# Gate and up of two swiglu layers by seven half-size products, and the rest of a product ahead of the next weight split

## The chip, the core and the metric

The kernel runs on one core of a Trainium2 chip. The core has a matrix engine (PE, TensorE), a vector engine (DVE), an activation engine (ACT), a general engine (POOL, GpSimd) and a queue engine (SP) that issues most loads. The metric is the device time of one execution in microseconds; less is better.

## The reference, cut to what matters

Two blocks of a transformer over 512 tokens of width 1024, all in float32. The first block holds two swiglu layers of inner width 2816 around a mixer; the second has an even and an odd mixer, each followed by a squared-relu MLP of inner width 4096.

```python
def rmsnorm(x, g):
    y = xf * lax.rsqrt(jnp.mean(xf * xf, axis=-1, keepdims=True) + EPS)
    return (y * g)
def swiglu(h, w_gu, w_down):
    g, u = jnp.split(h @ w_gu, 2, axis=-1)
    return (jax.nn.silu(g) * u) @ w_down
# first block
x = x + 0.5 * rmsnorm(swiglu(rmsnorm(x, g_pre_ffn1), w_gu1, w_down1), g_post_ffn1)
x = x + mixer(...)
x = x + 0.5 * rmsnorm(swiglu(rmsnorm(x, g_pre_ffn2), w_gu2, w_down2), g_post_ffn2)
# second block, twice (even mixer, odd mixer)
x = x + mixer(...)
x = x + sq_relu_mlp(rmsnorm_2(x, norm_mlp), w_mlp1, w_mlp2)   # relu(h @ w1) ** 2 @ w2
```

## The kernel before, in words

**Tiling.** Activations stand as 128 features by 512 tokens a tile. Each float32 operand is kept in two parts, hi (rounded) and lo (the remainder), and a product of a 128x128 weight tile with an activation tile is three matmuls: hi by hi, lo by hi, hi by lo. In the code these are the three lines L2158, L2160 and L2162 (512 tokens each) for a whole product, and L2176, L2178 and L2180 (256 tokens each) for a half-size one.

**Weights.** The weights arrive in one stream, cut in chunks of mostly eight 128x128 tiles (128x1024). For each chunk ACT writes `whi` (L2463) and DVE writes `wlo` (L2807). The ring of these buffers has NW = 4 places, so the chunk at place c + 4 can be split only once the PE is done with the chunk at c. `opened(key)` puts the splits up to c + 3 into the order just ahead of the product on chunk c.

**A planner writes the order.** `work_order` builds one list of steps by hand-written loops; each engine executes its share of the list in that order, in order, with semaphore waits. What stands earlier in the list is therefore ahead on every engine.

**Swiglu layers** (`ffn`, key `gate`). A half layer has 11 gate and 11 up tiles, each one chunk of 8 k-tiles (24 matmuls of 512), then 8 down tiles of 11 k-tiles. The token factor of the norm, `rb`, is multiplied into gate and up on DVE (L2925, L2927), silu is on ACT (L2530), gate times up on POOL (L3332), the hi and lo parts of the result are written by ACT (L2533) and DVE (L2929). While half 0 runs, `extra` puts one step of the rotary tables between two pairs of tiles.

**MLP layers by seven** (`mlp`). In the two MLP layers of the second block, 28 of the 32 inner tiles are already computed in blocks of four tiles by seven products of half the tokens instead of eight: 8 k-slices by 3 matmuls of 256 tokens each. A block's products run in the order q1, p5, p6, q2, q7, then q1 of the next block, then q4 and q3. They need sums of token halves (`token_sums`, tiles `thi`, `tlo`: L2467, L2472 on ACT, L2818 to L2828 on DVE) and sums of weights (DVE L2811 and three accumulating loads by POOL L3326). Between products the result of one is copied out of its bank (`hold`, ACT L2481) or added to a held one (`corner_sum`, DVE L2839); a finished quarter (`corner`) goes through relu L2489, square L2492 and its hi part L2497 on ACT, and its lo part L2852 on DVE; for quarter c22 DVE does relu and square in one (L2845). p6 waits for q1's hold, q7 for p6's hold, q4 for the sum of c22, q3 for p5's hold. A half of an MLP layer runs three (half 0) or four (half 1) such blocks.

**The order inside a block before.** `multiplied` first calls `product`, which opens the chunk (so puts the next split) and puts the matmuls, and then `later()`, the rest of the product before (its corner work):

```python
at_once, then = product(f, name, (*afree, ...) if f == 12 else afree)
later()
...
at_once()
```

## Time and profile before

| | |
|---|---|
| runs | 2422.3, 2423.24, 2423.79 us |
| median | 2423.24 us |
| the profiled execution | 2421.31 us, of which the span is 2419.5 us |
| mean granted PE clock | 0.995 |
| PE busy | 2366.7 us, 98% |
| PE weight loads busy | 1945.0 us, 80% |
| DVE busy | 1327.2 us, 55% |
| ACT busy | 1064.4 us, 44% |
| POOL busy | 232.8 us, 10% |

The order of the stages is: swiglu f1 until about 375 us, the mixer until about 940, swiglu f2 until about 1311, the even mixer until about 1455, the MLP 0 until about 1800, the odd mixer, and the MLP 1 with products by seven at about 2080 to 2150 and 2235 to 2320. A busy share is an average: what a stage waits for is read in that stage, from its start times and from what an instruction's idle time before it ended with. A matmul's recorded duration is longer than its place in the pipeline; the pace is the distance of start times.

### The profile page before, as it was taken

How to read it: one execution, taken by the hardware profiler on the slowest of the kernel's cores; microseconds unless marked ns; L12 is line 12 of the kernel's file. 1: busy time of each engine (PE TensorE's matmuls, PEld its weight loads, DVE VectorE, ACT ScalarE, POOL GpSimd, SP SyncE). 2: the span in 40 equal slices, each digit the busy share in tenths (PEclk: the TensorE clock that was granted, in tenths of full speed). 3: DMA queues.
4: the chain of work that ended last, by engine and by line, in shares of the span. 5: the costliest groups of instructions: out<-in, count | busy, mean ns of one | idle time of the engine just before them, and what ended most of it. 6: DMA issues, size and time to landing. Idle time of an engine off the chain costs nothing.

```text
span 2419.5 us, 30917 instructions
## 1 busy us (share of the span) xinstructions
PE 2366.7 (98%) x12252; PEld 1945.0 (80%) x12252; DVE 1327.2 (55%) x2135; ACT 1064.4 (44%) x1759; POOL 232.8 (10%) x189
## 2 busy tenths in 40 slices
PE   9999999999999999999999999999999999999998
PEld 8888888777777788888887667989987677888987
DVE  5533436788654345433335866735645676753653
ACT  4323224455432334322323456624624785741642
POOL 0100100322102010100100200001000100100100
PEclk9999999999999999999999999999999999999999
DMA  4323223211122131323222215536522112644641
GB/s 153 99 87 104 99 84 102 84 53 53 62 70 73 55 118 62 113 86 106 96 86 88 82 46 133 148 105 157 140 96 64 38 48 67 163 122 123 162 117 69
DMA packets 72864, 230.68 MB, mean 95 GB/s; under 512 B 8080, under 2 KB 16528, under 8 KB 72464
## 3 DMA queue, kind: packets, MB, share of 16 engines
q1 hardware_dynamic: 66384, 206.34, 26.0%
q0 software_dynamic: 6048, 22.02, 5.5%
q8 instruction: 97, 1.59, 0.3%
q14 instruction: 47, 0.39, 0.0%
q10 hardware_dynamic: 288, 0.34, 0.0%
HBM read 226.57 MB, written 2.10 MB: 95 GB/s over the span
## 4 chain that ended last, share of the span: by engine, by line
PE 84%; DVE 6%; ACT 5%; issue 3%; DMA 2%; POOL 0%; POOLq 0%; DVEq 0%; ACTq 0%
PE bank L2158 21%; PE bank L2162 21%; PE bank L2160 21%; PE bank L2176 3%; PE bank L2178 3%; PE bank L2180 3%; PE bank L2342 2%; DMA wraw<-in_stream 2%; ACT whi L2463 2%; PE bank L2304 1%; PE bank L2349 1%; DVE wlo L2807 1%; PE bank L2249 1%; PE bank L2245 1%; PE bank L2247 1%
## 5 line engine op out<-in xcount | busy, mean ns | idle before, releaser
L2807 DVE TENSOR_TENSOR wlo<-wraw,whi 128x1024 fp32r<-128x1024 f32 (+3 forms) x462 | 518.0, 1126 | 552.4 <-ACT whi L2463 551.6
L2463 ACT ACTIVATE whi<-wraw 128x1024 fp32r<-128x1024 f32 (+3 forms) x462 | 435.1, 948 | 470.4 <-PE bank L2162 377.0
L2158 PE MATMUL bank<-hhi,whi 128*128 128x512 f32 x1288 | 514.7, 400 | 2.3 <-ACT hhi L2508 1.0
L2162 PE MATMUL bank<-hhi,wlo 128*128 128x512 f32 x1288 | 504.1, 391 | 1.6 <-DVE wlo L2807 1.5
L2160 PE MATMUL bank<-hlo,whi 128*128 128x512 f32 x1288 | 503.3, 391 | 0.4 <-DVE hlo L2858 0.4
L2158 PEld LDWEIGHTS bank<-hhi,whi 128*128 128x128 f32 x1288 | 242.2, 188 | 56.6 <-issue 6.7
L2162 PEld LDWEIGHTS bank<-hhi,wlo 128*128 128x128 f32 x1288 | 241.7, 188 | 56.0 <-DVE wlo L2807 4.1
L2160 PEld LDWEIGHTS bank<-hlo,whi 128*128 128x128 f32 x1288 | 242.4, 188 | 50.0 <-DVE hlo L2858 2.6
L2160 PE MATMUL bank<-mlo,whi 128*128 128x512 f32 x448 | 176.8, 395 | 0.2 <-DVE mlo L3164 0.2
L2158 PE MATMUL bank<-mhi,whi 128*128 128x512 f32 x448 | 176.9, 395 | 0.0
L2162 PE MATMUL bank<-mhi,wlo 128*128 128x512 f32 x448 | 176.9, 395 | 0.0
L2176 PE MATMUL bank<-hhi,whi 128*128 128x256 f32 x448 | 126.9, 283 | 1.3 <-DVE tmps L2839 1.0
L2180 PE MATMUL bank<-hhi,wlo 128*128 128x256 f32 x448 | 126.9, 283 | 0.9 <-DVE wlo L2807 0.9
L2178 PE MATMUL bank<-hlo,whi 128*128 128x256 f32 x448 | 126.7, 283 | 0.0
L3332 POOL TENSOR_TENSOR tmps<-tmps 128x512 f32<-128x512 f32 x44 | 56.6, 1286 | 612.0 <-DVE tmps L2927 464.6
L2160 PEld LDWEIGHTS bank<-mlo,whi 128*128 128x128 f32 x448 | 84.2, 188 | 20.3 <-DVE mlo L3164 0.5
L2162 PEld LDWEIGHTS bank<-mhi,wlo 128*128 128x128 f32 x448 | 84.2, 188 | 20.1
L2158 PEld LDWEIGHTS bank<-mhi,whi 128*128 128x128 f32 x448 | 84.2, 188 | 19.8 <-ACT mhi L2659 0.4
L2176 PE MATMUL bank<-thi,whi 128*128 128x256 f32 x336 | 95.9, 285 | 1.8 <-ACT whi L2463 1.6
L2180 PE MATMUL bank<-thi,wlo 128*128 128x256 f32 x336 | 95.3, 284 | 1.5 <-DVE wlo L2807 1.5
L2645 ACT ACTIVATE tmps<-bank 128x512 f32<-128x512 f32 x88 | 52.8, 599 | 99.6 <-PE bank L2342 97.9
L2178 PE MATMUL bank<-tlo,whi 128*128 128x256 f32 x336 | 95.1, 283 | 0.0
(459 smaller groups left out, 4224.6 us busy)
## 6 DMA issues: line engine op xcount, KB each, us to landing
wraw<-in_stream SPq DMA_DIRECT2D x335, 512.0 KB, 3.4
wraw<-in_stream POOLq DMA_DIRECT2D x34, 512.0 KB, 6.0
wraw<-in_stream SPq DMA_DIRECT2D x32, 192.0 KB, 2.3
wraw<-in_stream SPq DMA_DIRECT2D x22, 256.0 KB, 2.6
rot_tables<-in_stream SPq DMA_DIRECT2D x8, 512.0 KB, 5.5
rot_tables<-in_stream POOLq DMA_DIRECT2D x8, 512.0 KB, 5.5
wraw<-in_stream SPq DMA_DIRECT2D x26, 128.0 KB, 2.0
wraw<-in_stream SPq DMA_DIRECT2D x8, 320.0 KB, 2.9
```

Source lines behind the costliest of these rows:

```text
L2158: pe.matmul(out, sh, xh, start=first, stop=False)
L2160: pe.matmul(out, sh, xl, start=False, stop=False)
L2162: p = pe.matmul(out, sl, xh, start=False, stop=end and last)
L2176: pe.matmul(out, sh, xh, start=fresh and n == 0, stop=False, skip_group_check=True)
L2178: pe.matmul(out, sh, xl, start=False, stop=False, skip_group_check=True)
L2180: p = pe.matmul(out, sl, xh, start=False, stop=n == 7, skip_group_check=True)
L2245: pe.matmul(out, xh, sh, start=k == 0, stop=False)
L2342: p = pe.transpose(banks[tb][:, i * 128:i * 128 + 128], src[:, at0:at0 + 128], ident[:, :])
L2463: act.activation(whi[j][:, 0:L], src[:, 0:L], F.Copy).then_inc(*hi.up(c))
L2645: act.activation(et_of(stage, et)[:, c * 128:(c + m) * 128], banks[tb][:, 0:m * 128], F.Copy).then_inc(*turned.up((stage, u, c)))
L2807: dve.tensor_tensor(wlo[j][:, 0:L], src[:, 0:L], whi[j][:, 0:L].bitcast(f32), SUB).then_inc(*lo.up(c))
L3332: pool.tensor_tensor(tmps[:, q, :], tmps[:, q, :], tmps[:, u, :], MUL).then_inc(*gated.up((s, f)))
```

## The change

**Swiglu layers.** Of the 22 gate and 22 up tiles of a layer, 4 pairs (`PLAIN` = 0, 1, 2, 11) stay whole products and come first; the other 18 pairs (`GATED`) are computed in 9 blocks of two gate and two up tiles by the seven half-size products of the MLP layers, in the same order of products. The token sums are made during the plain tiles, before the first block. `by_seven` holds what the MLP and swiglu layers share. Per block there is one DVE addition of weights and three accumulating POOL loads. The factor `rb` is multiplied into gate only (`gate_in`, `glu_gate`, DVE); up stays unscaled, and the later norm gets the factor through its EPS term, `eps_x` (both norms after the swiglu). silu stays on ACT; gate times up is on DVE for half of the tokens (`glu_first`) and on POOL for the other half (`glu_second`), where before all of it was on POOL. The steps of the rotary tables move from f1's half 0 to the down tiles of its half 1.

**All layers by seven, the two MLP layers too.** `multiplied` now calls `later()` ahead of `product`, so the rest of the product before stands ahead of the next split on ACT and on DVE.

On the PE 10481 rows become 11777: 1296 more, which is 2 layers by 9 blocks by (168 - 96).

```diff
+PLAIN, GATED = (0, 1, 2, 11), ((3, 5, 7, 9), (12, 14, 16, 18, 20))
...
-    def ffn(tag, gu, down):
+    def ffn(s, tag, gu, down_of):
+        lows[s], least = [], len(plan) + 2
+        for f in PLAIN:
+            col(tag + "g", gu + "g", f)
+            col(tag + "u", gu + "u", f)
...
-    ffn("f1", "gu1", "down1")
...
+            seven(tag + "s", s, GATED[half], lambda f: quadrants([gu + "g"] * 2 + [gu + "u"] * 2, (f, f + 1) * 2), down,
+                  least)
+            down(99)
+        order, n = [f for fs in GATED for f in fs], 0
+        for f, low in zip(order, lows[s]):
+            if f in (GATED[0][0], GATED[1][0]):
+                plan[CH_of(tag + "s", f, "p5") - 4].then.append(low)
+            elif f == GATED[0][1]:
+                plan[CH_of(tag + "s", order[n - 1], "p5")].then.insert(0, low)
+            else:
+                plan[CH_of(tag + "s", order[n - 1], "p6")].then.append(low)
+            n += 1
+    def CH_of(*key):
+        return [chunk.key for chunk in plan].index(key)
...
-    def gate(s, f, tg, tu, afree):
-        q, u = T.take(), T.take()
-        put("gate", s, f, tg.bank, tu.bank, q.i, u.i, tg.end, tu.end, (*q.was, *u.was), afree)
+    def gate_in(s, f, tg):
+        q = T.take()
+        put("gate_in", s, f, tg.bank, q.i, tg.end, q.was)
         tg.freed(("g_scaled", (s, f)))
-        tu.freed(("u_scaled", (s, f)))
-        u.free = (("gated", (s, f)),)
+        return q
+    def gate_up(s, f, tu, q):
+        put("gate_up", s, f, tu.bank, q.i, tu.end)
+        tu.freed(("combined", ("gated", s, f)))
+    def gate_low(s, f, q, afree):
+        put("gate_low", s, f, q.i, afree)
         q.free = (("v_lo", (s, f)),)
...
-    def ffn(s, tag, nxt, natural, afree, yfree, extra):
...
+    def by_seven(s, tag, afree_of, corner, first_time=None):
...
+        def product(f, name):
+            key = (s, f)
...
+            c = opened((tag, f, name))
+            put("seven", s, name, c, b.i, was, fresh)
+            closed.add(c)
+            done = ("used", c)
...
+            return at_once, lambda: corner(f, name, b, bank[f, "q"] if name != "q4" and (f, "q") in bank else None, done,
+                                           afree_of(f))
+        def multiplied(fs, tiles, owed):
...
+            for f, name in products(fs):
+                if name == "down":
+                    next(tiles[0])
+                    next(tiles[0])
+                    later()
+                    later = nothing
+                    continue
+                later()
+                at_once, then = product(f, name)
+                if first_time and (f, name) == first_time[0:2]:
+                    put(*first_time[2])
+                at_once()
+                state["held"] = False
+                later = then
+                if not first_time or f > first_time[0]:
+                    next(owed, int)()
+            next(tiles[1])
+            next(tiles[1])
+            later()
+            return ("used", CH[(tag, fs[-1], "q3")])
+        return multiplied
+    def ffn(s, tag, nxt, natural, guard, yfree, extra):
...
-        sy = None
+        afree, sy = guard, None
+        silu_of, wait_lo = {}, []
+        def corner(f, name, b, q, done, free):
+            key = (s, f)
+            if name == "q2":
+                silu_of[f] = q
+                put("glu_gate", key, "c11", q.i)
+            elif name == "q7":
+                silu_of[f, "up"] = q
+            elif name == "q4":
+                q = silu_of[f]
+                put("glu_first", key, b.i, q.i, done, free)
+                b.free = (("combined", (key, "c21")),)
+                wait_lo.append((key, "c21", q))
+            elif name == "q3":
+                u = silu_of[f, "up"]
+                put("glu_gate", key, "c12", q.i)
+                put("glu_second", key, q.i, u.i)
+                low()
+                u.free = (("gated", (key, "c12")),)
+                wait_lo.append((key, "c12", q))
+            elif name == "p6":
+                low()
+        def low():
+            if wait_lo:
+                key, part, q = wait_lo.pop(0)
+                put("glu_low", key, part, q.i, afree)
+                q.free = (("v_lo", (key, part)),)
+        multiplied = by_seven(s, tag + "s", lambda f: afree, corner)
         for half in range(2):
...
-                                              fresh=s > 0)
-                g2 = run(feat([(tag + "g0", 2, 0)], ("h", s)))
+                g0, u0, g1, u1 = side_by_side(("h", s), *[(tag + c, n, 0) for n in range(2) for c in "gu"], fresh=s > 0)
+                token_sums(s, 0, guard)
+                token_sums(s, 1, guard)
+                g2 = run(feat([(tag + "g", 2, 0)], ("h", s)))
                 R.step()
-                gate(s, 0, g0, u0, afree)
-                gate(s, 1, g1, u1, afree)
...
+                q0, q1 = gate_in(s, 0, g0), gate_in(s, 1, g1)
+                gate_up(s, 0, u0, q0)
+                gate_up(s, 1, u1, q1)
+                q2 = gate_in(s, 2, g2)
+                gate_low(s, 0, q0, afree)
+                gate_low(s, 1, q1, afree)
+                u2 = run(feat([(tag + "u", 2, 0)], ("h", s)))
+                token_sums(s, 2, guard)
+                gate_up(s, 2, u2, q2)
+                gate_low(s, 2, q2, afree)
+                g3 = run(feat([(tag + "g", 11, 0)], ("h", s)))
+                token_sums(s, 3, guard)
+                q3 = gate_in(s, 11, g3)
+                u3 = run(feat([(tag + "u", 11, 0)], ("h", s)))
+                put("token_last", s, u3.end)
+                gate_up(s, 11, u3, q3)
+                gate_low(s, 11, q3, (("p_lo", ("last token", s)),))
...
+            begun = [tile(0), tile(1)]
+            h_end = multiplied(GATED[half], begun, iter(()))
+            while wait_lo:
+                low()
...
-                tiles = feat([(tag + f"d{half}", n, k0) for k0, _ in groups(11)], ("v", s, half * 11))
+                if half and n < 5:
+                    next(extra, None)
+                    next(extra, None)
+                tiles = begun[n] if n < 2 else tile(n)
...
-            put("rotary", n)
+            put("rotary", n, (("lo", CH["f1s", GATED[1][-1], "q7"]), *ang.was, *kq.was) if n == 0 else ())
...
-        def multiplied(fs, tiles, afree):
-            def nothing():
-                pass
-            later = nothing
...
-                    continue
-                at_once, then = product(f, name, (*afree, *open_sums["h", s].tok) if f == 12 else afree)
...
-                    put("token_last", s, ("used", CH[(f"m{l}u", 3, 0)]))
-                at_once()
-                state["held"] = False
-                later = then
-                if f > 4:
...
+        multiplied = by_seven(s, f"m{l}s", lambda f: (*afree, *open_sums["h", s].tok) if f == 12 else afree, corner,
+                              (4, "p5", ("token_last", s, ("used", CH[(f"m{l}u", 3, 0)]))))
...
+            eps_x = lsm[:, 32:36]
...
                     w.wait_ge(*var[norm])
+                    if norm in (("h", 0), ("h", 2)):
+                        dve.tensor_scalar(eps_x, v, EPS, None, MUL).then_inc(*chain.up())
...
                     last_norm = norm
-                    dve.tensor_scalar(v, banks[b][:, 0:4], 1.0 / n, EPS, MUL, ADD).then_inc(*var.up(norm))
+                    if norm in (("y", 0), ("y", 2)):
+                        dve.scalar_tensor_tensor(v, banks[b][:, 0:4], 1.0 / n, eps_x, MUL, ADD).then_inc(*var.up(norm))
...
+                elif k == "gate_up":
+                    s, f, b, q, end = a
+                    w.wait_ge(*at(end))
+                    w.wait_ge(*silu[s, f])
+                    dve.tensor_tensor(tmps[:, q, :], banks[b][:, :], tmps[:, q, :],
+                                      MUL).then_inc(*combined.up(("gated", s, f)))
...
+                elif k == "glu_gate":
+                    key, part, q = a
+                    w.wait_ge(*rbm["h", key[0]])
+                    w.wait_ge(*combined[key, part])
+                    dve.tensor_tensor(two(tmps[:, q, :]), two(tmps[:, q, :]), twice_rb(part),
+                                      MUL).then_inc(*g_scaled.up((key, part)))
+                elif k == "glu_first":
+                    key, b, q, done, afree = a
+                    w.wait_ge(*at(done))
+                    w.wait_ge(*silu[key, "c11"])
+                    dve.scalar_tensor_tensor(tmps[:, q, :], banks[b][:, :], -1.0, tmps[:, q, :], MUL,
+                                             MUL).then_inc(*combined.up((key, "c21")))
...
-                    w.wait_ge(*silu[s, f])
-                    w.wait_ge(*u_scaled[s, f])
+                elif k == "glu_second":
+                    key, q, u = a
+                    w.wait_ge(*silu[key, "c12"])
+                    w.wait_ge(*combined[key, "c22"])
                     w.wait_ge(*before.now())
```

In this diff the ACT parts of the steps are left out: `gate_in` and `glu_gate` are silu, `gate_low` and `glu_low` write the hi part (L2630 to L2645 of the changed kernel), as before. In the changed kernel the line numbers of common steps are: split L2563 (ACT) and L2921 (DVE), hold L2581, corner L2589, L2592, L2597, plain copy for token sums L2567, `thi` L2572, `rb` L2617.

**ACT in MLP 0, one block by seven, from the product after q2 on.** L2489, L2492, L2497 are relu, square and hi part of a corner, L2463 is a split and L2481 a hold; `mhi0` is the hi part of the MLP's inner tiles. Before:

```order
L2463 ACTIVATE whi3<-wraw0_1 128x1024
L2489 ACTIVATE tmps<-tmps 128x512
L2492 ACTIVATE tmps<-tmps 128x512
L2497 ACTIVATE mhi0<-tmps 128x2x256
L2463 ACTIVATE whi0<-wraw0_0 128x1024
L2497 ACTIVATE mhi0<-tmps 128x2x256
L2481 ACTIVATE ftmps<-bank 128x512
L2463 ACTIVATE whi1<-wraw0_0 128x1024
L2463 ACTIVATE whi2<-wraw0 128x1024
L2489 ACTIVATE tmps<-bank 128x512
L2492 ACTIVATE tmps<-tmps 128x512
L2497 ACTIVATE mhi0<-tmps 128x2x256
```

After, with L2589, L2592, L2597 for the corner, L2563 for a split, L2581 for a hold:

```order
L2589 ACTIVATE tmps<-tmps 128x512
L2592 ACTIVATE tmps<-tmps 128x512
L2597 ACTIVATE mhi0<-tmps 128x2x256
L2563 ACTIVATE whi1<-wraw0_1 128x1024
L2597 ACTIVATE mhi0<-tmps 128x2x256
L2563 ACTIVATE whi2<-wraw0_0 128x1024
L2581 ACTIVATE ftmps<-bank 128x512
L2563 ACTIVATE whi3<-wraw0_0 128x1024
L2589 ACTIVATE tmps<-bank 128x512
L2592 ACTIVATE tmps<-tmps 128x512
L2597 ACTIVATE mhi0<-tmps 128x2x256
```

The split of q3's chunk stood ahead of the corner of q2 and now stands behind it; the splits of p5 and of p6 of the next block stood together behind the hold of q1, and now p5's stands ahead of that hold, with the corner of c22 ahead of it.

**ACT in f1, from the first plain tiles on.** L2530 is silu with its table load, L2533 the hi part, L2517 the copy of `rb`. Before:

```order
L2463 ACTIVATE whi2<-wraw0 128x1024
L2463 ACTIVATE whi3<-wraw1 128x1024
L2517 ACTIVATE rb<-bank 128x512
L2530 ACT_TABLE_LOAD
L2530 ACTIVATE tmps<-tmps 128x512
L2533 ACTIVATE f1ahi<-tmps 128x512
L2530 ACTIVATE tmps<-tmps 128x512
L2533 ACTIVATE f1ahi<-tmps 128x512
L2463 ACTIVATE whi0<-wraw0 128x1024
L2530 ACTIVATE tmps<-tmps 128x512
L2533 ACTIVATE f1ahi<-tmps 128x512
```

After, from the third of four steps of token sums to the first hold (L2630 silu, L2636 hi part, L2567 and L2572 token sums, L2577 the last token sums' hi part):

```order
L2567 ACTIVATE tmps<-xa,cols 128x512 x2
L2572 ACTIVATE f1thi<-ftmps 128x3x256
L2636 ACTIVATE f1ahi<-tmps 128x512
L2563 ACTIVATE whi1<-f1wraw_0 128x1024
L2567 ACTIVATE tmps<-xa,cols 128x512 x2
L2572 ACTIVATE f1thi<-ftmps 128x3x256
L2630 ACTIVATE tmps<-tmps 128x512
L2563 ACTIVATE whi2<-f1wraw_0 128x1024
L2577 ACTIVATE hhi<-f1t4 128x4x256
L2636 ACTIVATE f1v11hi<-tmps 128x512
L2563 ACTIVATE whi3<-wraw0 128x1024
L2581 ACTIVATE ftmps<-bank 128x512
```

Two steps of token sums, a split, the copy of `rb`, the table load, three silus, two hi parts and the split of q1's chunk stand ahead of the first row of this piece. The first hold of a block (q1's, its last row) stands behind all four steps of token sums and behind the hi part of the last plain tile.

## Rows read from the trace of the kernel before

**Rows 1.** The page: busy us (share of the span) and instructions.
```profile
PE 2366.7 (98%) x12252; PEld 1945.0 (80%) x12252; DVE 1327.2 (55%) x2135; ACT 1064.4 (44%) x1759; POOL 232.8 (10%) x189
```

**Rows 2.** Windows: stretch, PE, PEld, DVE, ACT, POOL busy, clock, DMA share, GB/s.
```profile
1080.00:1140.00 60.00, 60.00 (x260) 48.52 (x259) 15.64 (x16) 17.26 (x23) 0.00 (x0) 1.00 0.34 108
1680.00:1740.00 60.00, 60.00 (x479) 58.83 (x478) 40.16 (x46) 41.08 (x57) 4.35 (x5) 1.00 0.64 160
```

**Rows 3.** Matmul groups: ns min/median/max, first and last start us (f2 down tiles).
```profile
L2158 PE MATMUL bank<-f2ahi,whi x176: 392/394/398, 1068.1 to 1310.3; 128*128 128x512 f32 x176
```

**Rows 4.** The same view, half-size products of MLP 0, half 1.
```profile
L2176 PE MATMUL bank<-hhi,whi x128: 277/283/283, 1653.5 to 1738.9; 128*128 128x256 f32 x128
L2176 PE MATMUL bank<-thi,whi x96: 279/282/285, 1656.4 to 1727.6; 128*128 128x256 f32 x96
```

**Rows 5.** Timeline of DVE, MLP 0 half 1: start us, us, instruction, idle before it.
```profile
1685.76 0.68 DVE L2839 TENSOR_TENSOR tmps<-bank,ftmps 128x512 f32<-128x512 f32 x1
...
1689.42 1.23 DVE L2807 TENSOR_TENSOR wlo<-wraw,whi 128x1024 fp32r<-128x1024 f32 x1 [0.66 <-ACT whi L2463]
1690.57 1.22 DVE L2811 TENSOR_TENSOR wraw<-wraw,wraw 128x1024 f32<-128x1024 f32 x1
1691.70 0.69 DVE L2845 SCALAR_TENSOR_TENSOR tmps<-tmps 128x512 f32<-128x512 f32 x1
```

**Rows 6.** Timeline of ACT, the same stretch.
```profile
1686.48 0.64 ACT L2489 ACTIVATE tmps<-tmps 128x512 f32<-128x512 f32 x1
...
1688.35 1.04 ACT L2463 ACTIVATE whi<-wraw 128x1024 fp32r<-128x1024 f32 x1
1692.42 0.63 ACT L2497 ACTIVATE mhi<-tmps 128x512 fp32r<-128x512 f32 x1 [3.03 <-DVE tmps L2845]
1692.96 0.58 ACT L2481 ACTIVATE ftmps<-bank 128x512 f32<-128x512 f32 x1
1693.43 2.00 ACT L2463 ACTIVATE whi<-wraw 128x1024 fp32r<-128x1024 f32 x2
1695.33 0.59 ACT L2489 ACTIVATE tmps<-bank 128x512 f32<-128x512 f32 x1
```

**Rows 7.** Matmul groups of MLP 0, half 0.
```profile
L2176 PE MATMUL bank<-thi,whi x72: 279/282/415, 1498.8 to 1558.4; 128*128 128x256 f32 x72
```

**Rows 8.** Timeline of DVE in MLP 0, half 0.
```profile
1513.12 0.68 DVE L2839 TENSOR_TENSOR tmps<-bank,ftmps 128x512 f32<-128x512 f32 x1
...
1546.14 0.15 DVE L2872 TENSOR_SCALAR sm<-bank 128x4 f32<-128x4 f32 x1
...
1548.19 1.22 DVE L2807 TENSOR_TENSOR wlo<-rot_tables,whi 128x1024 fp32r<-128x1024 f32 x1
```

**Rows 9.** Groups of DVE instructions in 1513 to 1556 us: busy us, mean ns.
```profile
L2863 DVE TENSOR_TENSOR ssb<-ssb,xa 128x512 f32<-128x512 f32 x7 | 4.8, 683 | 0.0
```

**Rows 10.** Timeline of PE and windows, MLP 0 half 0: a wait, and the clock behind it.
```profile
1543.94 1.05 PE L2268 MATMUL bank<-ones,ssb 128*128 128x1 f32 x8 [1.50 <-DVE ssb L2863]
...
1546.00:1549.00 3.00, 3.00 (x18) 0.56 0.97 225
```

**Rows 11.** Timeline of ACT and PE at the start of f1, and of ACT in f2.
```profile
32.61 1.06 ACT L2463 ACTIVATE whi<-wraw 128x1024 fp32r<-128x1024 f32 x1 [3.11 <-DMA wraw<-in_stream]
...
39.90 1.28 ACT L2530 ACT_TABLE_LOAD   x1
...
39.00 0.48 PE L2158 MATMUL bank<-hhi,whi 128*128 128x512 f32 x1
...
970.01 1.06 ACT L2463 ACTIVATE whi<-wraw 128x1024 fp32r<-128x1024 f32 x1 [3.11 <-DMA wraw<-in_stream]
...
975.50 0.48 PE L2158 MATMUL bank<-hhi,whi 128*128 128x512 f32 x1
```

**Rows 12.** Timeline of ACT, token sums of MLP 0.
```profile
1484.44 1.32 ACT L2467 ACTIVATE tmps<-ya,cols 128x512 f32<-128x512 f32 x2
...
1487.68 1.05 ACT L2463 ACTIVATE whi<-wraw 128x1024 fp32r<-128x1024 f32 x1
```

More of the change, by code:

```diff
@@ L173, in stream_plan @@
             add(("eo", n, half), "e_out", 4 * half, 4, n * 128, 128)
-    def CH_of(*key):
-        return [chunk.key for chunk in plan].index(key)
     def mlp(l):
@@ new lines, in gate_up, with token_sums @@
+    def gate_up(s, f, tu, q):
[3 more added lines that the diff above has]
+        put("gate_low", s, f, q.i, afree)
+        q.free = (("v_lo", (s, f)),)
+    first, both = FT.slots
+    def token_sums(s, k, guard):
+        qs = [T.take(), T.take()]
+        for q, j in zip(qs, (k, k + 4)):
+            put("plain", s, j, q.i, (*q.was, *x_at[j]))
+        put("token_sums", s, k, qs[0].i, qs[1].i, (*first.free, *both.free), guard)
+        for q in qs:
+            q.free = (("combined", ("token", s, k, 4)),)
+        put("token_parts", s, k, guard)
+        first.free = both.free = (("p_hi", ("token", s, k)), ("p_lo", ("token", s, k)))
@@ new lines, in ffn, with tile @@
+                token_sums(s, 3, guard)
[4 more added lines that the diff above has]
+                gate_low(s, 11, q3, (("p_lo", ("last token", s)),))
+            def tile(n):
+                return feat([(tag + f"d{half}", n, k0) for k0 in (0, 8)], ("v", s, half))
+            begun = [tile(0), tile(1)]
+            h_end = multiplied(GATED[half], begun, iter(()))
@@ L967, in work_order @@
     last, owed = None, 0.0
-    first, second = ([dil_unit(p, i) for i in range(4)] for p in range(2))
-    for unit in first + [None] + second + [None]:
+    ones_of, twos_of = ([dil_unit(p, i) for i in range(4)] for p in range(2))
+    for unit in ones_of + [None] + twos_of + [None]:
         pace = 1 if unit else 5
@@ L1182, in mlp @@
         put(*lows[s][0])
-        first, both = FT.slots
         def square(t, f, afree):
@@ L1189, in square @@
             q.free = (("v_lo", (s, f)),)
-        def token_sums(k):
-            qs = [T.take(), T.take()]
-            for q, j in zip(qs, (k, k + 4)):
-                put("plain", s, j, q.i, (*q.was, *x_at[j]))
-            put("token_sums", s, k, qs[0].i, qs[1].i, (*first.free, *both.free), guard)
-            for q in qs:
-                q.free = (("combined", ("token", s, k, 4)),)
-            put("token_parts", s, k, guard)
-            first.free = both.free = (("p_hi", ("token", s, k)), ("p_lo", ("token", s, k)))
         def one_more_split():
@@ new lines, in corner @@
+        def corner(f, name, b, q, done, free):
+            part = {"q2": "c11", "q7": "c22", "q4": "c21", "q3": "c12"}.get(name)
+            if part is None:
+                if name == "p6":
+                    low()
+                return
+            key = (s, f)
+            if part == "c21":
+                q = T.take()
+                put("corner", key, part, b.i, q.i, (done, *q.was), free)
+                b.free = (("relu_sq", (key, part, "relu")),)
+            else:
+                put("corner", key, part, None, q.i, (), free)
+            low()
+            wait_lo.append((key, part, q))
@@ L2022, in three, with twice_rb @@
             return v.rearrange("q (n t) -> q n t", n=3)
+        def twice_rb(part):
+            p = slice(0, 256) if part in ("c11", "c21") else slice(256, 512)
+            return rb[:, p].unsqueeze(1).to_broadcast([128, 2, 256])
         def two(v):
@@ L2027, in corner_of @@
         def corner_of(s, f, part):
-            f0, p = f % 16 + (2 if part in ("c11", "c12") else 0), slice(0, 256) if part in ("c11", "c21") else slice(256, 512)
-            a, b = v_tile(s, f0, 2)
+            p = slice(0, 256) if part in ("c11", "c21") else slice(256, 512)
+            if s < 3:
+                a, b = (v[:, f % 11:f % 11 + 2, :] for v in ahl[s])
+            else:
+                a, b = v_tile(s, f % 16 + (2 if part in ("c11", "c12") else 0), 2)
             return a[:, :, p], b[:, :, p]
```

208 lines of the change are left out of this document (99 added, 109 removed).

## The prediction

> **What bounds the kernel now.** First the page: the PE is busy 98% of the span, DVE 55%, ACT 44% [rows 1]. Fewer PE instructions' time should then shorten the kernel one for one, as long as ACT and DVE keep up where work is added to them. So I read two windows next. In the down tiles of f2 the weight loads fill 48.5 of 60 us and ACT 17 us; in a stretch of products by seven in MLP 0 the weight loads fill 58.8 and ACT and DVE 41 and 40 of 60 us [rows 2]. That is two thirds busy, yet their work is a chain: ACT writes a hi part, DVE the lo part, and each in its order. Whether such a chain fits into a block is the question in both kinds of layer. The timelines of the two engines in that stretch give its steps.
>
> **The PE's gain.** The pace of a 512-token matmul is (1310.3 - 1068.1) / 1053 = 0.2300 us, where 1053 is the intervals between: 176 groups of three on f2's down tiles and the 22 tiles of 24 of half 1 that stand among them, 528 + 528 - 3 [rows 3]. For half-size products, 224 groups of three stand between 1653.5 and 1738.9, 669 intervals, with 24 whole matmuls among them: (85.4 - 24 x 0.23) / 669 = 0.1194 us [rows 4]. A block of two gate and two up tiles is 96 x 0.2300 = 22.08 us before and 168 x 0.1194 = 20.06 us after, 2.02 less. Times 18 blocks: **-36.4 us**. A product by seven is 24 x 0.1194 = 2.87 us.
>
> The trace shows 0.2300 and 0.1194 us a matmul at a granted clock of 1.00 [rows 2 to 4]. The Trainium skill ("TensorE: Matmul & The Clock Gate", Back-to-back issue gap) gives a gap of N / 2.4 + 2.5 ns, so 215.8 and 109.2 ns. By that page's figures a block would go from 20.72 to 18.34 us and the gain would be an estimated 42.8 us, 6.4 more. The rows here are 7% and 9% above it, so the trace differs and decides.
>
> **The MLP layers: the order of corner and split.** Nothing is added there, but in the order of ACT the corner of a product now stands ahead of the next split. I walked one block with the intervals of the rows, from the sum of c11 on DVE (behind q2). Sum to relu 0.72 (1685.76 to 1686.48), relu, square and hi part to the next split 1.87 (to 1688.35) [rows 5, 6]. Split to its lo part on DVE 1.07 (to 1689.42), lo part to the next DVE work 1.15 (to 1690.57) [rows 5, 6]. Now the sum of c22: it stood in front of that lo part in time before, and now comes behind it. To its square 0.63, to the hi part on ACT 0.72 (1691.70 to 1692.42), to the split of p5's chunk 0.54, to its lo part 1.07, to the addition of weights 1.15, addition to the split of p6's chunk 1.25 (its 1.22 and a signal), that split 0.95 (a half of the pair's 1.90, 1693.43 to 1695.33), corner of c21 and the split of q2's chunk 1.87, its lo part 1.07, sum of c12 1.15, relu 0.72, corner and split of q7's chunk 1.87, next 0.95, the hold of p5 0.48 (1692.96 to 1693.43), the split of the next q1 to its lo part 1.07, that lo part, the lo part of a corner and one more weight's lo part 1.15 + 0.60 + 1.15, and the next sum of c11 is there. The sum is **23.2 us a block, in which the PE does not occur, against 20.06 us of the PE**. Before, the splits of p5 and p6 were issued together (the pair at 1693.43) and q3's ahead of the corner [rows 6], and the PE held the pace.
>
> In half 1 (four blocks) the way from the first sum of c11 to the last q7 is two blocks and, to the end of the hold of p6, 18.75 + 0.48 + 0.95 + 0.5 = 20.7: 2 x 23.2 + 20.7 = 67.1 against 3 x 20.06 = 60.2, so +6.9 in each MLP. In half 0 (three blocks) the first sum of c11 stands at 1513.12 [rows 8]. One block and 20.7 lead to 1557.0. Seven additions of squares (0.60 of place each, 4.2) and the root of the norm (1546.14 to 1548.19, 2.05) also stand on DVE there [rows 8, 9]; of these 6.25 I put 4.7 on the way, for those that stand between a lo part and the sum behind it: 1561.7. Before, the last product on token sums began at 1558.4 - 23 x 0.1194 = 1555.7 [rows 7]. So +6.0. Two MLPs: 2 x (6.9 + 6.0) = **+25.8 us**. The bounds: 0, if ACT has hidden time that the walk counts as bound, and 2 x (9.3 + 7.5) = 33.6 if nothing of the slack at the start of a half is there.
>
> **The clock.** Behind a wait of 1.50 us of the PE in MLP 0 the granted clock is 0.56 for 3 us [rows 10], that is a time at 1.2 GHz; about 1.3 us are lost. New stalls of 2 to 3 us a block can do this again; I take it twice, **+2.6 us** (0 to 12 x 1.3 = 15.6).
>
> **The swiglu blocks in their steady run.** The same walk with the work of a swiglu block: there is no relu and square pair, c21 and c12 need one DVE multiplication and one silu or none, and the hi parts are written a product later. It comes to about 19.3 us, under 20.06, so the PE holds the pace with 0.8 us in hand: 0. If that is lost, it is a rival (below). On POOL `glu_second` waits for the silu of c12, and behind it in POOL's order stand the accumulating loads of the next block's weight sums; what they feed is split three products (8.6 us) later, so I cost that wait at nothing too, and at a split that comes late if silu were over 8 us late.
>
> **The first block of each swiglu layer.** Here ACT has the four token steps as well. The last split before is at 32.61 [rows 11]. A token step takes 3.24 us on ACT, with its wait for DVE (1484.44 to 1487.68) [rows 12]. From 33.56, two steps lead to 40.0, a split to 41.0, the copy of rb to 41.6, the table load (1.28) [rows 11] to 42.9. Three silus, each between a DVE multiplication with rb and one with up, and two hi parts lead to the split of q1's chunk at 47.2; the third step and a hi part to p5's split at 53.7; lo part and addition end at 57.1, the fourth step and the last silu at 61.3, where p6's chunk is split; the last token sums' hi part 62.2; the hi part of tile 11, which waits for DVE and the end of the last up tile, 65.3; q2's split 65.9; then q1's hold, 66.8 to 67.4. The PE: the up tile 2 starts at 39.00 [rows 11], three tiles of 24 x 0.23 lead to 55.5, q1 and p5 to 61.2. p6 needs q1's hold: a stall of 6.2 us. In f2 the split is at 970.01 and the up tile at 975.50 [rows 11]: 5.49 apart instead of 6.39, so 7.1 us. Together **+13.3 us**. The bounds: ACT's work alone is five splits, four steps, silus, hi parts and the copies, an estimated 25.6 us by the durations of rows 6, 11 and 12, to 59.2 from 33.56 on, which would be no stall; with every wait it is 8 us a layer.
>
> **The rest** I cost at nothing. EPS times the variance is one DVE instruction on 4 columns a layer, like the one of 0.15 us that opens a root [rows 8]. The rotary steps move to down tiles, where ACT and DVE have 17 and 16 of 60 us of work [rows 2], so they are covered; uncovered, five double steps would be a few us. 18 more additions of weights and 54 accumulating loads: MLP 0 runs the same at a DMA share of 0.64 [rows 2].
>
> **The sum**, against the profiled execution: 2421.3 - 36.4 + 13.3 + 2.6 + 25.8 = 2426.6. The median of the runs is 1.9 above the profiled one (2423.24 against 2421.31): **2428 us**.
>
> **The rivals.** (a) The MLP walk is too long: ACT and DVE run ahead at the block's start and the PE keeps its pace; only the start stalls stay. 2421.3 - 36.4 + 13.3 + 2.6 + 1.9 = 2403. For it speaks that ACT and DVE are two thirds busy [rows 2]; against it that every step of the walk is a row. 0.12. (b) The MLPs bind, but the first blocks' stalls are hidden, since the waits for DVE are shorter than walked: 2428 - 13.3 - 1.3, about 2413. 0.18. (c) Neither binds: 2387. 0.04. (d) Slower: the swiglu loop, 0.8 us under the PE's pace in my walk, is over it by 0.8 us on average, as two signals of 0.8 would do; 16 blocks x 0.8, and the clock falls in some of them: 2428 + 15 = 2443. It decides from a chain over 20.06 us a block. For it: the two loops differ by four instructions only. 0.14.
>
> **How the numbers follow.** The forecast, 2428 with its own range of 2419 to 2438, has 0.52. From 2404 to 2441 no more than 2 in 10 is left out: most of (a) is at the lower edge, half of (d) is above. A measurement here can tell 0.2%, 4.8 us: faster is under 2418.4: (a), (c) and most of (b), 0.31. Within: 2418.4 to 2428.1, half of the forecast and the rest of (b), 0.31. Slower: the other half and (d), 0.38.
>
> **What would show it.** In f2's blocks, L2276 starts 20.1 us a block apart and no idle time of the PE. In MLP 0's half 1, blocks 23 us apart, the PE idle twice a block, ended by ACT's hold (L2581) and by DVE or ACT behind the sum of c22; ACT's rows between with short idle times ended by DVE. At about 61 us and 997 us one idle time of the PE of 6 to 7 us, ended by ACT L2581. The clock row near 1.00 elsewhere. The forecast is wrong if MLP 0's half 1 takes 85 us as before, or if the f1 blocks are over 20.5 us each.

## The result and the profile after

The changed kernel takes 2485.12 us, the kernel before 2423.24 us: a ratio of 1.0253, 95% interval 1.0241 to 1.0264. It is 62 us slower where 5 us slower was forecast, and outside the range.

The page of the changed kernel, in its first row, the row of its second DMA queue and the row of the chain that ended last, by engine; below it the same row of the kernel before:

```profile
PE 2366.4 (95%) x13548; PEld 2004.4 (81%) x13548; DVE 1470.2 (59%) x2287; ACT 1158.9 (47%) x1892; POOL 245.7 (10%) x217
...
q0 software_dynamic: 13824, 50.34, 11.7%
...
PE 69%; DVE 10%; ACT 9%; DMA 6%; issue 6%; POOL 0%; POOLq 0%; ACTq 0%; DVEq 0%
```

```profile
PE 84%; DVE 6%; ACT 5%; issue 3%; DMA 2%; POOL 0%; POOLq 0%; DVEq 0%; ACTq 0%
```

The PE was at 98% [rows 1] and is at 95%: 117 us without it, where there were 53. Its busy time is the same to 0.3 us although it has less to do: part of it runs at the lower clock. The share of DMA in the chain went from 2% to 6%, and those of DVE and ACT nearly doubled. The second row is the queue of the accumulating loads: 50 MB, 22 MB before.

Where the time went can be read from the starts of one group of matmuls that both programs have at every norm (L2279 before, L2379 after): at the end of f1 378.06 before and 385.54 after, at the end of f2 1314.56 and 1329.12. The stretches are cut at these starts.

| stretch | before, us | after, us | difference |
|---|---|---|---|
| f1 | 339.87 | 347.40 | +7.5 |
| the first block's mixer | 563.93 | 562.63 | -1.3 |
| f2 | 372.57 | 380.95 | +8.4 |
| even mixer's norm | 33.08 | 33.13 | 0 |
| even mixer and MLP 0 | 486.92 | 513.14 | +26.2 |
| odd mixer and MLP 1, half 0 | 296.76 | 306.86 | +10.1 |
| MLP 1 to its last norm | 277.79 | 290.25 | +12.5 |

The two swiglu layers, which were to gain, lost 16 us, and the stretches of the two MLP layers, which had their order changed only, 49 us. Two kinds of wait stand in the PE's timeline after (start, duration, instruction, idle time before it and what ended it), at the start of a swiglu layer, in a steady swiglu block, and in MLP 0, half 1:

```profile
67.56 0.55 PE L2276 MATMUL bank<-f1thi,whi 128*128 128x256 f32 x1 [5.47 <-ACT ftmps L2581]
...
1011.37 0.55 PE L2276 MATMUL bank<-f2thi,whi 128*128 128x256 f32 x1 [5.45 <-ACT ftmps L2581]
...
102.79 0.36 PE L2276 MATMUL bank<-hhi,whi 128*128 128x256 f32 x1 [1.91 <-DVE tmps L2953]
...
125.01 0.36 PE L2276 MATMUL bank<-hhi,whi 128*128 128x256 f32 x1 [1.93 <-DVE tmps L2953]
...
274.65 0.36 PE L2276 MATMUL bank<-hhi,whi 128*128 128x256 f32 x1 [2.85 <-DVE tmps L2953]
...
1723.26 0.55 PE L2276 MATMUL bank<-hhi,whi 128*128 128x256 f32 x1 [4.73 <-DVE tmps L2953]
...
1749.78 0.55 PE L2276 MATMUL bank<-hhi,whi 128*128 128x256 f32 x1 [4.78 <-DVE tmps L2953]
```

The first two are q1's hold, the start stall of the prediction. The others are q4 waiting for the sum of c22 (L2953). In the MLP they were forecast, at some 3 us a block. In the steady swiglu blocks they were not, and 11 of them leave the PE idle for 18.0 us. They cost an estimated 20 us: idle time is counted from the recorded end of a matmul, 0.28 us after its start, and the pace is 0.12 us, so each wait costs some 0.16 us more than it shows. The chain that ended last in the MLP explains both. Its pieces from one such wait to the next, in order of time (start, us, what):

```profile
1696.43 0.69 DVE tmps L2953
1697.15 0.70 DVE tmps L2959
1697.90 0.52 issue
1698.41 1.05 ACT whi L2563
1699.53 1.10 issue
1700.63 1.23 DVE wraw L2925
...
1704.76 0.96 ACT whi L2563
1705.74 1.24 DVE wlo L2921
1707.00 8.38 DMA wraw<-in_stream
1715.40 1.07 ACT whi L2563
1716.53 1.11 issue
1717.63 0.69 DVE tmps L2953
```

This is my walk of one block, sum of c22 to split of p5, to the addition, to the split of q2's chunk and its lo part. But behind the lo part there is not the sum of c12: there is a load of 8.38 us. In the code of the plan, the weight tiles b (of q2) and d (of q4) of a block use the same raw buffer in turn. When DVE has written the lo part of q2's chunk, SP may load d, and d must have landed for the split of q4's chunk, three products (8.6 us) later in the order. From q2's lo part to the next sum of c11 it is 11.9 us (1705.74 to 1717.63) this way, where my way over the sum of c12, two splits and a hold had 9.1. A block takes 26.5 us (1749.78 less 1723.26). ACT, which works in order, waits for the load:

```profile
1715.40 1.06 ACT L2563 ACTIVATE whi<-wraw 128x1024 fp32r<-128x1024 f32 x1 [2.96 <-DMA wraw<-in_stream]
1718.35 0.63 ACT L2589 ACTIVATE tmps<-tmps 128x512 f32<-128x512 f32 x1 [1.89 <-DVE tmps L2953]
```

The chain in f1 has the same load, between 86.41 and 95.50 us (9.1 us) and again between 109.03 and 117.72 (8.7 us). Over that stretch of the MLP the median load of 512 KB by SP lands after 3.7 us; the one in the chain takes over twice that.

The kernel before has this load too. It is issued at 1696.91, beside the accumulating loads of its block, and lands at 1703.65, after 6.7 us. ACT's split waits for it, but only briefly, and the PE not at all:

```profile
1703.67 1.06 ACT L2463 ACTIVATE whi<-wraw 128x1024 fp32r<-128x1024 f32 x1 [0.67 <-DMA wraw<-in_stream]
```

### The profile page after: what moved, and what is told of

It reads as the page before. It is cut to its first block, busy times and chain, and to the rows that moved or that the text cites. A ratio compares the mean times of both kernels' runs of the same rounds, so it can differ in the third digit from the quotient of the medians.

```text
span 2483.9 us, 33903 instructions
## 1 busy us (share of the span) xinstructions
PE 2366.4 (95%) x13548; PEld 2004.4 (81%) x13548; DVE 1470.2 (59%) x2287; ACT 1158.9 (47%) x1892; POOL 245.7 (10%) x217
## 4 chain that ended last, share of the span: by engine, by line
PE 69%; DVE 10%; ACT 9%; DMA 6%; issue 6%; POOL 0%; POOLq 0%; ACTq 0%; DVEq 0%
PE bank L2258 15%; PE bank L2262 15%; PE bank L2260 15%; DMA wraw<-in_stream 6%; PE bank L2276 4%; ACT whi L2563 4%; PE bank L2280 4%; PE bank L2278 4%; DVE wlo L2921 2%; PE bank L2442 2%; DVE tmps L2953 1%; PE bank L2404 1%; PE bank L2449 1%; PE bank L2349 1%; PE bank L2345 1%
## 5 line engine op out<-in xcount | busy, mean ns | idle before, releaser
L2921 DVE TENSOR_TENSOR wlo<-wraw,whi 128x1024 fp32r<-128x1024 f32 (+4 forms) x442 | 496.0, 1124 | 528.3 <-ACT whi L2563 527.5
L2563 ACT ACTIVATE whi<-wraw 128x1024 fp32r<-128x1024 f32 (+4 forms) x442 | 415.6, 943 | 424.7 <-PE bank L2262 262.5
L2276 PE MATMUL bank<-hhi,whi 128*128 128x256 f32 x1024 | 300.4, 293 | 50.3 <-DVE tmps L2953 45.3
L2280 PE MATMUL bank<-hhi,wlo 128*128 128x256 f32 x1024 | 297.9, 291 | 1.0 <-DVE wlo L2921 1.0
L2278 PE MATMUL bank<-hlo,whi 128*128 128x256 f32 x1024 | 298.1, 291 | 0.0
L2258 PE MATMUL bank<-hhi,whi 128*128 128x512 f32 (+1 forms) x712 | 290.9, 409 | 1.7 <-ACT hhi L2608 1.0
L2262 PE MATMUL bank<-hhi,wlo 128*128 128x512 f32 (+1 forms) x712 | 280.1, 393 | 3.4 <-DVE wlo L2921 3.4
L2260 PE MATMUL bank<-hlo,whi 128*128 128x512 f32 (+1 forms) x712 | 279.2, 392 | 0.4 <-DVE hlo L2972 0.3
L2258 PEld LDWEIGHTS bank<-hhi,whi 128*128 128x128 f32 (+1 forms) x712 | 134.1, 188 | 34.0 <-issue 5.4
L2260 PEld LDWEIGHTS bank<-hlo,whi 128*128 128x128 f32 (+1 forms) x712 | 134.3, 189 | 27.6 <-DVE hlo L2972 2.9
```

The source lines that it names most:

```text
L2258: pe.matmul(out, sh, xh, start=first, stop=False)
L2260: pe.matmul(out, sh, xl, start=False, stop=False)
L2262: p = pe.matmul(out, sl, xh, start=False, stop=end and last)
L2276: pe.matmul(out, sh, xh, start=fresh and n == 0, stop=False, skip_group_check=True)
L2278: pe.matmul(out, sh, xl, start=False, stop=False, skip_group_check=True)
L2280: p = pe.matmul(out, sl, xh, start=False, stop=n == 7, skip_group_check=True)
```

## The experiments

**Theory A**: the order is the cause; with the corner ahead of the split, each lo part comes later, and the reload of d closes a loop over both engines and the queue. **Theory B**: the added work in the swiglu layers binds whatever the order. **Theory C**: the reload is long only because the accumulating loads of the same moment share the DMA engines with it.

**e1: the old order everywhere.**

```diff
-                later()
                 at_once, then = product(f, name)
+                later()
```

> The changed kernel with the order of before in all layers by seven: product (and its split) first, then the rest of the product before. Theory A (the order of corner and split closes a loop through the raw buffer's reload, in swiglu and MLP alike): the MLPs lose the 48.8 us they gained, the steady stalls of the swiglu blocks go, the two stalls of 6 to 7 us at their start stay with their clock: 2423.2 - 36.4 + 13.3 + 5 = about 2405 us. Theory B (in the swiglu layers the added ACT, DVE and load work binds whatever the order): the MLPs come back, the swiglu layers stay 16 us longer than before: about 2437 us.

Measured: 2422.73 us, ratio 1.0003 (0.9993 to 1.0012). The MLPs came back (MLP 0's stretch 487.3 us, before 486.9), and the waits for the sum of c22 in the swiglu blocks went. So the order was the MLP loss, but for 3 us (from the end of f2 to the last norm 1097.3 us, before 1094.6). But the swiglu layers reached only 2.3 us under before, not 18. What is left there is the start stall, as in the changed kernel, and at four of f1's and five of f2's blocks a wait of over 0.5 us of this kind:

```profile
67.61 0.55 PE L2276 MATMUL bank<-f1thi,whi 128*128 128x256 f32 x1 [5.47 <-ACT ftmps L2581]
...
260.02 0.36 PE L2276 MATMUL bank<-f1thi,whi 128*128 128x256 f32 x1 [0.92 <-ACT ftmps L2581]
```

It lies between A's 2405 and B's 2437, and neither holds as it stood: A is right on the large waits, and the small ones, which stay in the old order, it did not have.

**e2: the new order alone, in the kernel before.**

```diff
-                at_once, then = product(f, name, (*afree, ...) if f == 12 else afree)
                 later()
+                at_once, then = product(f, name, (*afree, ...) if f == 12 else afree)
```

> The kernel before with one edit: in the two MLP layers the rest of a product stands ahead of the next split; swiglu layers as before. Theory A: the whole MLP loss of the changed kernel, +48.8 us: about 2472 us, with waits of some 4.8 us of the PE a block for the sum of c22. My prediction's walk alone (ACT and DVE, no load in the loop) says +28: 2451 us. If the MLP loss came from something the swiglu part changed (buffers, tables, placing), no change: 2423 us.

Measured: 2464.6 us, ratio 1.017 (1.0154 to 1.0186), +43 us. The two lines do by themselves nearly all that the MLPs lost; my walk without a load (+28) is too short by 15 us. The waits are those of the changed kernel:

```profile
1705.22 0.55 PE L2176 MATMUL bank<-hhi,whi 128*128 128x256 f32 x1 [4.72 <-DVE tmps L2839]
```

**e3: the old order in the MLPs only.**

```diff
-                later()
+                if s < 3:
+                    later()
                 at_once, then = product(f, name)
+                if s > 3:
+                    later()
```

> The changed kernel with the old order in the two MLP layers only; the swiglu layers keep the rest of a product ahead of splits. Theory A: 2485.1 - 48.8 = about 2436 us, and 16 us over before in the swiglu layers stay. If the losses of the two kinds of layer are not additive (clock, shared queues): outside 2432 to 2440.

Measured: 2440.64 us, ratio 1.0077 (1.0059 to 1.0095). That is 4.6 us over the forecast and just over the band given: the losses of the two kinds of layer add up but for a few us. e3 less e1 is what the new order costs in the swiglu layers, 18 us.

**e4: the same order, small accumulating loads.** 7/8 of every weight sum is left out.

```diff
-                    pool.dma_start(raw_at(r)[:, :], in_stream(plus), accum_op=ADD).then_inc(...)
+                    pool.dma_start(raw_at(r)[:, 0:128], in_stream(plus)[:, 0:128], accum_op=ADD).then_inc(...)
```

> The changed kernel with each accumulating load of a weight sum cut from 1024 columns to 128, so that 7/8 of every weight sum is left out; order and waits are the same. Theory C (the reload in the loop is long only because the accumulating loads of the same moment share the DMA engines: 9 us instead of 4 to 5): the loop falls by about 4 us a block, under 20.1 us in the swiglu layers (16 us of loss there go) and to the ACT and DVE walk of 23 us in the MLPs (their loss from 48.8 to about 28): about 2485 - 16 - 20 = 2449 us. If the loads' sharing does not matter: 2485 us.

Measured: 2437.25 us, ratio 1.0063 (1.0044 to 1.0082): 48 us less than the changed kernel, with the same instructions in the same order. It shows what was added on the queue side and what my walk was worth. Windows of 60 us in f1 (half 0, half 1) and in MLP 0, half 1; columns as in [rows 2]; first the changed kernel, then e4:

```profile
90.00:150.00 60.00, 56.16 (x434) 54.76 (x433) 39.74 (x42) 28.31 (x38) 7.04 (x8) 0.97 0.55 139
230.00:290.00 60.00, 55.40 (x450) 55.05 (x450) 40.86 (x43) 28.67 (x38) 11.74 (x12) 0.97 0.71 175
1690.00:1750.00 60.00, 49.73 (x399) 49.08 (x398) 33.31 (x37) 32.13 (x45) 5.25 (x6) 0.95 0.55 141
```

```profile
90.00:150.00 60.00, 60.00 (x479) 58.81 (x478) 41.70 (x46) 29.41 (x40) 6.95 (x7) 1.00 0.33 95
230.00:290.00 60.00, 60.00 (x505) 60.00 (x504) 45.58 (x48) 32.35 (x43) 10.88 (x11) 1.00 0.37 106
1680.00:1740.00 60.00, 55.88 (x421) 53.91 (x420) 37.00 (x42) 37.34 (x52) 4.34 (x5) 0.97 0.35 103
```

In the swiglu blocks the PE is busy throughout and the clock stays at 1.00: the ACT and DVE loop is under 20.06 us, as walked (how far under, the run does not tell). In the MLP it is not. Two waits for the sum of c22, one block apart, stand 23.21 us from each other, where the walk gave 23.2:

```profile
1685.10 0.48 PE L2276 MATMUL bank<-hhi,whi 128*128 128x256 f32 x1 [1.95 <-DVE tmps L2953]
...
1708.31 0.36 PE L2276 MATMUL bank<-hhi,whi 128*128 128x256 f32 x1 [1.43 <-DVE tmps L2953]
```

The reload of f1's chain (9.1 and 8.7 us) takes 4.2 us in e4 (issued at 86.26 and landed at 90.43, then at 106.68 and 110.91).

The rest of ACT's idle time before a split of a plain weight (L2563 on `wraw`, 60 to 150 us) names the difference. The changed kernel, then e4 (count, busy us, mean ns, idle before by releaser):

```profile
L2563 ACT ACTIVATE whi<-wraw 128x1024 fp32r<-128x1024 f32 (+1 forms) x14 | 14.2, 1016 | 10.2 <-DMA wraw<-in_stream 4.2 <-PE bank L2262 4.1 <-PE bank L2280 1.9
```

```profile
L2563 ACT ACTIVATE whi<-wraw 128x1024 fp32r<-128x1024 f32 (+1 forms) x16 | 15.8, 986 | 9.4 <-PE bank L2280 5.1 <-PE bank L2262 4.1
```

With small sums no split waits for a reload; in the changed kernel two do, 4.2 us. What is not shown by itself is the shared buffer: no run gives b and d a buffer each. That it is the link is read from the chain and the code.

**e11: the new order in the kernel before, with small accumulating loads** (e2 with e4's edit; 7/8 of every weight sum is left out).

> The kernel of e2 (before, with the rest of a product ahead of the next split in the MLPs) with each accumulating load cut from 1024 columns to 128; 7/8 of every weight sum is left out. If the loss of e2 (+42.8) is my walk of ACT and DVE (25.8 + 2.6) plus a reload that shares the DMA engines with the accumulating loads, the walk's part is left: 2423 + 25 to 28 = about 2450 us. If the reload is all of it: 2423 us. If the sharing plays no part in the MLPs: 2465 us.

Measured: 2448.06 us, ratio 1.0113 (1.0097 to 1.0129), +27 us. The MLP loss splits: 27 us are there with small loads, where the loop is one of ACT and DVE, as the prediction had it (25.8 + 2.6), and the other 16 us of e2 with the full size of the accumulating loads. The sum fits piece by piece as well: half 1 of the two MLP layers is 7.0 and 7.5 us longer than before (forecast 6.9 each), and the blocks are 23.21 us apart:

```profile
1702.14 0.36 PE L2176 MATMUL bank<-hhi,whi 128*128 128x256 f32 x1 [1.98 <-DVE tmps L2839]
...
1725.35 0.36 PE L2176 MATMUL bank<-hhi,whi 128*128 128x256 f32 x1 [1.44 <-DVE tmps L2839]
```

where e2 had a wait of 4.72.

**e9: the old order and small sums, in the changed kernel** (e1 with e4's edit; 7/8 of every weight sum is left out).

> The kernel of e1 with each accumulating load cut from 1024 columns to 128; 7/8 of every weight sum is left out. With the old order the ACT and DVE chains do not bind and with small sums the loads do not either: the small waits of the swiglu blocks (0.6 to 1.1 us, ended by ACT's hold) go, MLPs as before: before - 30.4 (the PE's gain with the gate and up tiles' own pace of 0.2266) + 13.7 (start stalls) + 3 (clock) = about 2409 us. If those waits are of the order itself: 2420 us.

Measured: 2404.64 us, ratio 0.9927 (0.9912 to 0.9942), 4 us under its forecast. The small waits that e1 kept are gone; of the swiglu layers' waits only those at their start are left (5.5 us in each layer, and up to 0.6 us ahead of it). So those small waits needed the full-size accumulating loads too, which is a piece of theory B. But the forecast was met in part by an offset. The two swiglu layers are 11.9 us shorter than before, where it had 13.7. And the stretches of the MLP layers, which it took as before, are 7 us shorter (1087.2 against 1094.6), all of it in the two stretches from a mixer to the end of half 0. Small loads help there in the old order too: these stretches take 199.1 and 291.9 us, and in e1, with full-size loads, 202.0 and 298.5. In half 1 they do not (285.3 and 277.8 us, before 285.7 and 277.8). So of e2's 16 us over e11 the 10 us that lie in half 1 of the two layers need the new order and the full-size loads together; for the rest this is not shown.

**e5: q1's hold ahead of the last plain tile's hi part**, on e1.

```diff
-        multiplied = by_seven(s, tag + "s", lambda f: afree, corner)
+        hook = [GATED[0][0], "p5", None]
+        multiplied = by_seven(s, tag + "s", lambda f: afree, corner, hook)
...
-                gate_low(s, 11, q3, (("p_lo", ("last token", s)),))
+                hook[2] = ("gate_low", s, 11, q3.i, (("p_lo", ("last token", s)),))
+                q3.free = (("v_lo", (s, 11)),)
```

> The kernel of e1 (old order) with the hi and lo part of the last plain tile moved behind q1's hold in both swiglu layers. If the start stall is the chain on ACT up to that hold, as the prediction walked it, the hold comes 2.5 to 3 us earlier and the stall of 5.6 us falls to about 3 us in each layer: 2422.7 - 5 to 7 = about 2416 us. If the stall is set by something else (the sum of p6's weights, the token sums), no change: 2422.7 us.

Measured: 2415.56 us, ratio 0.9973 (0.9963 to 0.9982): 0.3% or 7 us less than e1 by the ratios, at the long end of the forecast. The start stall is shorter by the 2.7 us that the hi part and its wait had taken:

```profile
65.96 0.36 PE L2278 MATMUL bank<-f1thi,whi 128*128 128x256 f32 x1 [2.76 <-ACT ftmps L2583]
```

**e6: the token sums earlier**, on e5. Two steps in f1 and one in f2 go into ACT's idle time during the first four tiles, the others close up.

```diff
         open_sums[R.next].pay()
+        if sums and x == ("h", 0):
+            next(sums)
         for n in range(len(keys)):
             ...
+            if sums and n == 1:
+                next(sums)
...
+                sums = (token_sums(s, k, guard) for k in range(4))
-                token_sums(s, 0, guard)
-                token_sums(s, 1, guard)
+                next(sums)
+                next(sums)
...
-                token_sums(s, 2, guard)
+                next(sums, None)
...
-                token_sums(s, 3, guard)
```

> The kernel of e5 with the token sums put earlier, into idle time of ACT during the first four tiles (two steps earlier in f1, one in f2). If the prediction's account of the start (25.6 us of ACT work and its waits) is right, both start stalls go with their clock losses of 1 to 3 us each: 2422.7 - 13 to 17 = about 2407 us. If the weight sum of p6 is late behind them, 2 us a layer are left: 2411 us.

Measured: 2410.53 us, ratio 0.9952 (0.9935 to 0.997). f1's start stall is gone. f2 keeps one of 1.78 us and has a new wait of 1.25 us at a plain tile (ended by DVE), so the time is nearer to the 2411 that was given for a rest than to 2407. Whether it is the late sum for p6 that is left, as the forecast had it, no run shows.

**e10: the new order at one product only**, on e6: p5 of the swiglu blocks. There the next split (q7's chunk) waits for an accumulating load, and silu of c12 and the hi part of c21 need not stand behind it.

```diff
+                if s < 3 and name == "p5":
+                    later()
+                    later = nothing
                 at_once, then = product(f, name)
                 later()
```

> The kernel of e6 with the order of the change at one product only, p5 of the swiglu blocks: silu of c12 and the hi part of c21 ahead of the split of q7's chunk, which waits for an accumulating load. If the small waits left in e6 (0.6 to 1.0 us at nine of 18 blocks, ended by ACT's hold of p6) come from these two instructions standing behind that split, they go: 2410.5 - 5 to 7 = about 2405 us. If the hold is late because of the load itself, no change: 2410 us; if the lo parts behind come later by it, slower.

Measured: 2400.73 us, ratio 0.992 (0.9905 to 0.9936), better than forecast and the fastest of the complete kernels. This wait stood in e6 at some ten blocks:

```profile
252.70 0.36 PE L2283 MATMUL bank<-f1thi,whi 128*128 128x256 f32 x1 [0.54 <-ACT ftmps L2588]
```

In e10 f1's steady blocks have none, at full-size loads and a DMA share of 0.72 in both windows:

```profile
70.00:130.00 60.00, 59.99 (x503) 59.81 (x502) 44.81 (x49) 32.04 (x42) 10.83 (x11) 1.00 0.72 176
220.00:280.00 60.00, 60.00 (x505) 60.00 (x504) 45.51 (x49) 33.07 (x43) 11.75 (x12) 1.00 0.72 176
```

So a high DMA share is not itself a loss. It becomes one where a load is a link of the loop. Nor did the loads get faster: with three accumulating loads under way at its issue, a 512 KB load of SP takes 6.4 to 8.6 us in e10 (15 loads).

## Why the prediction was wrong, point by point

**The PE's gain, -36.4: mis-sized by 6.** I took the pace of the down tiles for the gate and up tiles too. Their own rows in the kernel before are these (first the gate and up tiles, then the down tiles):

```profile
L2158 PE MATMUL bank<-hhi,whi x165: 389/389/389, 200.0 to 311.5; 128*128 128x512 f32 x165
```

```profile
L2158 PE MATMUL bank<-f1ahi,whi x88: 392/394/398, 312.9 to 373.8; 128*128 128x512 f32 x88
```

111.5 / 492 = 0.2266 us and 60.9 / 261 = 0.2333 us. The span of [rows 3] ran over both kinds and gave their mean, 0.2300. A block of gate and up tiles was 21.75 us, the gain is 1.69 a block and 30.4 in all. The check: e4's swiglu layers, where nothing but the start stalls and their clock is left, are 13.0 us shorter than before (7.1 and 5.9 by the same matmul's starts), and -30.4 + 13.5 + 3.4 for the clock (by its windows) is -13.5.

**The first blocks' stalls, +13.3: right.** Measured 6.3 us in f1 (waits of 0.55 and 5.47, and 0.16 for each) and 7.2 us in f2 (0.67, 0.61 and 5.45), 13.5. That their cause was the chain up to q1's hold is shown by e5 and e6.

**The MLPs, +25.8: the mechanism right, one link missing.** The loop of ACT and DVE is over the PE's pace, and e11 measures 27 us and 23.21 us a block for it. The step that failed is "that lo part ... and the next sum of c11 is there": behind q2's lo part the raw buffer is loaded again for q4's split. I had priced every wait for an engine and none for a buffer to be refilled. From that lo part to the next sum of c11 the walk had 9.1 us, and with the load in it 11.9 were measured. The profile of before shows short waits of ACT for DMA in half 1 of the MLP layers, of 0.20 to 0.81 us (0.67 for this very load), which I passed over; they were loads with little time in hand. The rest of the loss is 22 us between e11's 27 and the 49 of the stretches: 16 of them come with the full-size loads (e2 less e11), and some 6 (49 less e2's 43) only in the whole changed kernel; by the stretches of the profiled executions these are 14 and 9. For the last part I have no run that tells its cause.

**The steady swiglu blocks, 0: wrong, +20 in waits.** The step that failed is "so the PE holds the pace with 0.8 us in hand". e4 shows that without full-size loads it does hold it (no wait at all), and that the same link was missing: in f1's first window ACT and DVE are busy 28 and 40 of 60 us, the loop is 22.2 us (the wait at 125.01 less the one before at 102.79) and 8.7 of them are the load. I had named the accumulating loads as the thing to look at and priced them at nothing by the DMA share alone (0.64 in MLP 0 [rows 2]). A share tells whether the engines have room, not how long one load takes beside others.

**The clock, +2.6: far too low.** Over windows of 10 us, (1 - granted clock) x 10 sums to 12.5 us before and 43.8 after. In the swiglu layers alone it goes from 1.7 to 17.0. Part of it lies in time in which the PE waited anyway; the swiglu layers' own account (-30.4 + 13.5 + 20 in waits against +16 measured) leaves 13 us for it there. My bound of 15.6 was per 12 stalls; there were over 20. A window of f1 with the wait of 1.93 us in it (stretch, PE busy, clock, DMA share, GB/s):

```profile
120.00:130.00 10.00, 8.07 (x55) 0.83 0.40 114
```

It shows 0.83, so a third of those 10 us was granted 1.2 GHz and the rest 2.4; the fall came after an idle time of 1.93 us.

**The rivals.** (d) came nearest: it has the swiglu loop over the PE's pace, but by signals of 0.8 us, and what closed it was a load. None had the load in it, and so the range ended 44 us too low. Of the Trainium skill's rule for the gap of a single matmul ("TensorE: Matmul & The Clock Gate", Back-to-back issue gap, 215.8 and 109.2 ns) the trace stays 5% and 9% above, with 226.6 and 119.4 ns; it erred as my own sum did, on the side of a larger gain.

## What to carry to other kernels

Walk a loop over its buffers too: for each buffer, from its last reader to the load into it, to the first reader, with the time that a load takes beside the loads of the same moment, and not its median alone. In a kernel that is bound by one engine, putting ready work ahead of a prefetch step on another engine is not neutral: it delays what the prefetch's end releases, so it must be placed product by product (e10 gained 8 us over e6 by the order that at every product cost 18). And a gain is priced with the pace of exactly those instructions that go.

## What the runs showed of the hardware

A matmul of 128x512 keeps a pace of 0.2266 us on one kind of operands and 0.2333 us on another in the same program, in uninterrupted streams at a clock of 1.00; why, no run here tells. A load of 512 KB by SP in the changed kernel took a median of 3.5 us when no accumulating load of POOL was under way with it, and 7.4 to 9.6 us when three of the same size were at its issue (16 loads); in the kernel before 3.4 and 6.2 to 6.7 us (6 loads). And the waits in the changed kernel's swiglu layers, 30.7 us of idle PE in pieces of 0.6 to 5.5 us, came with an estimated 13 us lost at the lower clock, while e6's, all under 2 us, left the clock of these layers at 1.00 in every window of 10 us. The length of a wait alone does not decide it: the changed kernel's clock fell behind one of 1.81 us (at 1172.79) and stayed at 1.00 behind one of 1.91 us (at 102.79).
